# Moving the last column tile of each layer's input projection behind the index matmuls, in a two-block transformer kernel

## The chip, the cores and the metric

The kernel runs on one core of a Trainium2 chip. The metric is the device time of one execution in microseconds, lower is better. Engines: TensorE (PE, matmuls; PEld its weight loads), VectorE (DVE), ScalarE (ACT), GpSimd (POOL) and SyncE (SP, which here only issues DMAs). Each engine works through its own queue in order, and waits on semaphores that the others raise.

## What is computed

A first transformer block (three attention branches, a recurrent branch, gates, a dense feed-forward) is followed by two layers of a second kind. The change is in those two layers. For 256 tokens of width 1024, each of them computes

```
h = x @ w_in                          # 1024 x 1892, split into
a_q a_k a_v  b_q b_k b_v  i_q i_k i_w  c_q c_kv c_kr
o_a: sliding-window attention of rope(a_q), rope(a_k), a_v
o_b: the indexer: score = sum_h i_w * relu(rope(i_q) . rope(i_k)); the 64 best keys
     of each query are kept; attention of rope(b_q), rope(b_k), b_v over those keys
o_c: q_c = rms_norm(c_q) @ w_uq, kv_c = rms_norm(c_kv) @ w_ukv, attention with rope parts
x = layer_norm(alpha*x + [o_a o_b o_c] @ w_out)
x = layer_norm(alpha*x + mixture_of_experts(x))
```

All in float32. Products are made of three matmuls of split operands: a value is rounded to a short form ("hi"), the rest is kept apart ("lo"), and hi*hi, hi*lo and lo*hi are added up.

## The kernel before

**Weight tiles.** All weights stream in tiles of 128 x 2048 through a ring of three buffers. SyncE loads a tile into `raw`, ScalarE rounds it into `whi` (`split_hi`, L1197 to L1202), VectorE writes the difference into `wlo` (`split_lo`, L1543 to L1547), TensorE uses both and raises `tile_used`. A rounding waits until the tile three places earlier has been used. The load of a tile waits until the tile three places earlier has been split by both engines.

**The input projection.** The 1892 columns of `w_in` are eight tiles of 256 columns (the last of 100) taken in the order `L_COLS = [0, 1, 2, 4, 5, 6, 7, 3]`: tile 3, columns 768 to 1023, is the B queries and comes last (j = 7). `cols_tile` (L739) makes one: 2 token halves x 8 depths x 3 matmuls = 48 matmuls into PSUM bank 0 or 1 by turns. ScalarE evicts each into `h` (`evac_h`, L1395) and raises `ring_free`. Tiles 8 and 9 of the layer's ring are the up projections of the C branch, tiles 10 to 13 `w_out`, 14 the router.

**The order of the work** is written out by hand, for each engine, and is the same in both layers:

- TensorE (L967 to L989): column tiles 0 to 5, transposes of the A queries (L955), tile 6, transposes of the A keys and the rest, tile 7 (the B queries), then the wait for the rope of the index queries and for the eviction of the previous transposes, the transposes of the index queries, the wait for their eviction, and eight index matmuls (L987), which contract over 64 rows. Then it waits for the relu (L1014) and goes through twelve attention units of scores (L794), transposes of the probabilities (L806) and values (L821); between them stand the transposes of the C input at unit 1, the up projections at units 2 and 3 (L992 to L1011), the C transposes at 5 and 6, and the B transposes at unit 8.
- ScalarE (L1412 to L1426): evictions of the column tiles and of the transposes (`block_out`, L1402), each followed by the rounding of the tile two places on; behind the eviction of tile 7 the eviction of the index transposes (block 2), the relu of the index matmuls in two activations (L1424, L1425), and the rounding of tile 10. Then exponentials and evictions of the units.
- VectorE (L1782 to L1820): the subtractions of tiles 2 to 9, the moments of the C input, its scaling (L1808, needs GpSimd's power L706), the subtraction of tile 10, and behind the relu the eight index scores (L1819, each waits for the one before). Then unit 0: logits (L1572, L1574), a step of the top-64 search (L1826, L1827), and at unit 1 the lo part of the C input (L1833), for which TensorE's up projection waits.
- GpSimd (L696 to L718): rope of A, of the index part, of the C key part, the power L706, then behind the eighth `ring_free` of the layer (that is, the eviction of tile 7) the rope of the B queries and keys (L709; L676 to L679 and copies L687), and much later the rope of the C queries.

```
                pool.wait_ge(ring_free, l * 8 + (N_COL + 8))
                rope(5, 64, C_CC, C_SS, cols(BQ, 5), 4, [(1, BK)])
```

Of the kernel before, what the change touches and what calls it, by code (L numbers as in the profile page):

```python
# [192 lines left out]
def build(nc, I, out):  # L193
    with ExitStack() as ctx:
# [8 lines left out]
        def banks(a, b):  # L203
            return ps[:, a:b, :].rearrange("p a b -> p (a b)")
# [522 lines left out]
        def _(pe):  # L727
# [211 lines left out]
            for l in range(LAYERS):  # L939
# [12 lines left out]
                def turns(items, k=P):  # L952

                    for b, src in enumerate(items):
                        x = pe.transpose(banks(2, 4)[0:k, b * P:(b + 1) * P], src, ident)  # L955
                    x.then_inc(tb_full, 1)
# [7 lines left out]
                def doubled(which):  # L964
                    return [twice[which][:, t, :] for t in range(TT)]

                for j in range(8):  # L967
                    if j >= 2:
                        pe.wait_ge(ring_free, l * 8 + (N_COL + j - 1))
                    cols_tile(T_L + j, v, (N_COL + j) % 2, L_WIDTHS[j], True, (1,) if j < 2 else (0, 1))  # L970
                    if j == 5:
                        pe.wait_ge(rope_done, l * 4 + 1)
                        turns(pairs(AQ, 3))
                    if j == 6:
                        tb_wait(1)
                        turns([h[:, t, AQ + 384:AQ + 512] for t in range(TT)] + doubled(2) + doubled(3))
# [5 lines left out]
                for t, o, w in ((1, banks(4, 6), S), (0, banks(6, 7), P)):  # L982
                    for x in (0, 2, 1, 3):
                        a = 64 * (x % 2)
                        if x == 1:
                            lk(ins)
                        ins = pe.matmul(o[:, x * w:(x + 1) * w], iq_t[a:a + 64, x // 2, t * P:(t + 1) * P],  # L987
                                        ik_t[a:a + 64, 0:w], start=True, stop=True)
                ins.then_inc(idx_full, 1)  # L989


                def up_queries():  # L992
# [201 lines left out]
        def _(act):  # L1194
# [188 lines left out]
            for l in range(LAYERS):  # L1383
# [25 lines left out]

                one = lambda x: x.rearrange("p (a b) -> p a b", a=1)  # L1410
                sizes = [KD * min(256, IN2 - t * 256) for t in L_COLS] + [768, 512, TW, TW, TW, TW, 128, TW, TW]
                for j in range(9):  # L1412
                    if j >= 1:
                        evac_h(j - 1)
                    if j == 6:
                        block_out(0, [(aq_t[:, 0:3, :], 0, 6)])
                    if j == 7:
                        block_out(1, [(aq_t[:, 3:4, :], 0, 2), (ak_t, 2, 4)])
                    if j < 8:
                        split_hi(T_L + j + 2, v, sizes[j + 2])  # L1420
# [2 lines left out]
                act.wait_ge(pv_full, l * U_PER + U_L0)  # L1423
                act.activation(relu_t[0], banks(4, 6), ACT.Relu)  # L1424
                act.activation(relu_t[1], banks(6, 7), ACT.Relu).then_inc(idx_relu, 1)  # L1425
                split_hi(T_L + 10, v)  # L1426
                nu = l * U_PER + U_L0
                for i in range(U_PER + 2):
# [614 lines left out]
```

## Time and profile before

| | |
|---|---|
| time, median of 3 runs | 1383.97 us (1383.74 to 1385.13) |
| the profiled execution's own time | 1379.53 us |
| its span | 1377.7 us |
| mean granted clock of TensorE | 0.917 of full speed |
| busy: TensorE, VectorE, ScalarE, GpSimd | 1192.6, 782.8, 586.9, 104.0 us |
| bytes moved by DMA | 215.87 MB |

The span runs from the first to the last instruction of the profiled execution; its own time has a little around it. Busy time is the time in which an engine executes something, waits excluded. All times in rows below are microseconds from the start of the span, unless marked ns. "The chain that ended last" goes back from the last instruction, at each step to what released it. The granted clock has two levels here, 1.00 (2.4 GHz) and 0.50 (1.2 GHz); a window with a value between them holds a change.

### The profile page before, as it was taken

The numbers are of one execution on the slowest core, as the hardware profiler recorded it, in microseconds if no ns is written. First come the engines' busy times: TensorE is split into PE (matmuls) and PEld (weight loads), VectorE is DVE, ScalarE is ACT, GpSimd is POOL, SyncE is SP. The second block draws the span as 40 slices with busy tenths as digits, with TensorE's granted clock in tenths as the row PEclk, the third lists the DMA queues.
The fourth block names the chain that finished last, engine by engine and source line by source line (L and its number), as shares of the span: only waits on it lengthen the run. The fifth ranks groups of instructions, "written<-read, shape, count | busy, mean of one in ns | idle before, by whom it ended". The sixth has DMA issues, their size and how long they took to land.

```text
span 1377.7 us, 17333 instructions
## 1 busy us (share of the span) xinstructions
PE 1192.6 (87%) x6958; PEld 1040.3 (76%) x6958; DVE 782.8 (57%) x946; ACT 586.9 (43%) x706; POOL 104.0 (8%) x151
## 2 busy tenths in 40 slices
PE   4999899997999989868859999887958858998885
PEld 4999899987999979747657876666936747886664
DVE  5344545775444455465355467766367454557775
ACT  3444445633333333344124456553334314446661
POOL 3000101000000002610000000000621000000000
PEclk9999999998999998857969999998975978999997
DMA  8644434562555553300134569882410006468990
GB/s 270 211 144 123 151 122 150 175 209 99 195 183 183 184 175 97 114 19 1 31 121 153 182 219 312 307 294 85 144 54 3 31 31 213 136 200 284 309 317 37
DMA packets 115077, 215.87 MB, mean 157 GB/s; under 512 B 9546, under 2 KB 79178, under 8 KB 115008
## 3 DMA queue, kind: packets, MB, share of 16 engines
q1 hardware_dynamic: 112432, 209.90, 46.2%
q0 software_dynamic: 1424, 4.59, 1.0%
q8 instruction: 48, 0.79, 0.2%
q10 hardware_dynamic: 1152, 0.42, 0.1%
q14 instruction: 21, 0.17, 0.0%
HBM read 213.80 MB, written 1.09 MB: 156 GB/s over the span
## 4 chain that ended last, share of the span: by engine, by line
PE 66%; DVE 13%; DMA 9%; ACT 7%; issue 3%; POOL 1%; SPq 1%; POOLq 0%; ACTq 0%; DVEq 0%
PE ps L735 15%; PE ps L737 15%; PE ps L736 14%; DMA raw<-in_w_up 6%; DVE wlo L1546 6%; ACT whi L1202 4%; PE ps L794 3%; PE ps L771 3%; PE ps L821 3%; PE ps L772 3%; PE ps L773 3%; DMA raw<-in_w_down 2%; PE ps L806 2%; PE ps L1079 1%; PE ps L1080 1%
## 5 line engine op out<-in xcount | busy, mean ns | idle before, releaser
L1546 DVE TENSOR_TENSOR wlo<-raw,whi 128x2048 fp32r<-128x2048 f32 (+1 forms) x199 | 445.9, 2243 | 323.5 <-ACT whi L1202 322.6
L1202 ACT ACTIVATE whi<-raw 128x2048 fp32r<-128x2048 f32 (+1 forms) x199 | 369.5, 1861 | 227.2 <-PE ps L737 112.5
L735 PE MATMUL ps<-act_hi,whi 128*128 128x256 f32 (+1 forms) x784 | 228.1, 291 | 11.0 <-DVE act_lo L1553 11.0
L736 PE MATMUL ps<-act_lo,whi 128*128 128x256 f32 (+1 forms) x784 | 226.0, 288 | 0.0
L737 PE MATMUL ps<-act_hi,wlo 128*128 128x256 f32 (+1 forms) x784 | 225.9, 288 | 0.0
L735 PEld LDWEIGHTS ps<-act_hi,whi 128*128 128x128 f32 (+1 forms) x784 | 152.2, 194 | 17.3 <-DVE act_lo L1553 12.6
L736 PEld LDWEIGHTS ps<-act_lo,whi 128*128 128x128 f32 (+1 forms) x784 | 152.1, 194 | 1.2
L737 PEld LDWEIGHTS ps<-act_hi,wlo 128*128 128x128 f32 (+1 forms) x784 | 152.0, 194 | 1.0
L735 PE MATMUL ps<-whi,moe_r 128*128 128x512 f32 x320 | 132.8, 415 | 18.2 <-DVE wlo L1546 17.9
L737 PE MATMUL ps<-whi,moe_r 128*128 128x512 f32 x320 | 128.6, 402 | 0.0
L736 PE MATMUL ps<-wlo,moe_r 128*128 128x512 f32 x320 | 128.2, 401 | 0.0
L735 PE MATMUL ps<-whi,act_hi 128*128 128x256 f32 (+1 forms) x336 | 98.3, 293 | 4.5 <-DVE act_lo L1553 4.5
L735 PE MATMUL ps<-whi,mix_hi 128*128 128x512 f32 (+1 forms) x172 | 70.8, 412 | 32.5 <-DVE mix_lo L1833 13.7
L737 PE MATMUL ps<-whi,act_lo 128*128 128x256 f32 (+1 forms) x336 | 97.4, 290 | 0.0
L736 PE MATMUL ps<-wlo,act_hi 128*128 128x256 f32 (+1 forms) x336 | 97.3, 290 | 0.0
L735 PEld LDWEIGHTS ps<-whi,moe_r 128*128 128x128 f32 x320 | 61.4, 192 | 39.5 <-DVE wlo L1546 19.2
L628 POOL TENSOR_TENSOR small<-small 128x1 f32<-128x1 f32 x14 | 7.7, 557 | 946.9 <-DVE small L1564 946.8
L794 PE MATMUL ps<-arena 64*128 64x256 f32 (+3 forms) x208 | 63.3, 427 | 10.8 <-ACT pbuf L1425 3.2
L737 PEld LDWEIGHTS ps<-whi,moe_r 128*128 128x128 f32 x320 | 61.2, 191 | 14.9
L736 PEld LDWEIGHTS ps<-wlo,moe_r 128*128 128x128 f32 x320 | 61.6, 193 | 13.0
L735 PEld LDWEIGHTS ps<-whi,act_hi 128*128 128x128 f32 x336 | 67.1, 200 | 5.3 <-DVE act_lo L1553 5.3
L735 PEld LDWEIGHTS ps<-whi,mix_hi 128*128 128x128 f32 x172 | 33.6, 195 | 47.2 <-DVE mix_lo L1833 15.1
(258 smaller groups left out, 1945.8 us busy)
## 6 DMA issues: line engine op xcount, KB each, us to landing
raw<-in_w_in SPq DMA_DIRECT2D x45, 1024.0 KB, 5.5
raw<-in_w_down SPq DMA_DIRECT2D x43, 1024.0 KB, 5.0
raw<-in_w_gate SPq DMA_DIRECT2D x64, 512.0 KB, 4.4
raw<-in_w_up SPq DMA_DIRECT2D x64, 512.0 KB, 5.2
raw<-in_w_gu SPq DMA_DIRECT2D x22, 1024.0 KB, 5.1
raw<-in_w_out SPq DMA_DIRECT2D x12, 1024.0 KB, 4.9
raw<-in_p_b SPq DMA_DIRECT2D x2, 1024.0 KB, 5.2
raw<-in_p_c SPq DMA_DIRECT2D x2, 1024.0 KB, 5.3
```

Source lines behind the costliest of these rows:

```text
L735: pe.matmul(o, ah, bh, start=first, stop=False)
L736: pe.matmul(o, ah, bl, start=False, stop=False)
L737: return pe.matmul(o, al, bh, start=False, stop=last)
L771: pe.matmul(o, a, cc, start=f, stop=False)
L772: pe.matmul(o, a, d, start=False, stop=False)
L773: x = pe.matmul(o, b, cc, start=False, stop=g)
L794: x = pe.matmul(o[:, i, :], u["q"][i], u["k"][i], start=True, stop=True)
L806: x = pe.transpose(o[:, b * P:(b + 1) * P], p[:, i, kt * P:(kt + 1) * P], ident)
L821: x = pe.matmul(oo, pt[:, b * P:(b + 1) * P], u["v"][i][kt], start=f, stop=g)
L1079: pe.matmul(o, xk_hi[:, t, k, :], put[:, t, a:b], start=t == 0, stop=False)
L1202: act.activation(whi[:, c % 3, 0:n], raw[:, c % 3, 0:n], ACT.Copy).then_inc(hi_made, 1)
L1546: dve.tensor_tensor(wlo[:, c % 3, 0:n], raw[:, c % 3, 0:n], whi[:, c % 3, 0:n].bitcast(F32), ALU.subtract)\
```

## The change

In each of the two layers, TensorE's seven first column tiles stay where they are, and the eighth (the B queries) is issued behind the eight index matmuls, ahead of the wait for the relu. ScalarE no longer evicts it in the loop, but behind the two relu activations and ahead of the rounding of tile 10. Nothing else is changed: GpSimd's rope of the B queries waits for the same count of evictions, VectorE's and SyncE's queues are as before. No instruction is added or removed.

```diff
@@ TensorE @@
-                for j in range(8):
+                def columns(j):
                     if j >= 2:
                         pe.wait_ge(ring_free, l * 8 + (N_COL + j - 1))
                     cols_tile(T_L + j, v, (N_COL + j) % 2, L_WIDTHS[j], True, (1,) if j < 2 else (0, 1))
+
+                for j in range(7):
+                    columns(j)
                     if j == 5:
                         pe.wait_ge(rope_done, l * 4 + 1)
                         turns(pairs(AQ, 3))
...
                         ins = pe.matmul(o[:, x * w:(x + 1) * w], iq_t[a:a + 64, x // 2, t * P:(t + 1) * P],
                                         ik_t[a:a + 64, 0:w], start=True, stop=True)
                 ins.then_inc(idx_full, 1)
+                columns(7)
@@ ScalarE @@
-                for j in range(9):
+                for j in range(8):
                     if j >= 1:
                         evac_h(j - 1)
                     if j == 6:
...
                 act.activation(relu_t[0], banks(4, 6), ACT.Relu)
                 act.activation(relu_t[1], banks(6, 7), ACT.Relu).then_inc(idx_relu, 1)
+                evac_h(7)
                 split_hi(T_L + 10, v)
```

## Rows read from the trace of the kernel before

**Rows 1.** The page: its head, and the chain's shares by engine.
```profile
span 1377.7 us, 17333 instructions
...
PE 66%; DVE 13%; DMA 9%; ACT 7%; issue 3%; POOL 1%; SPq 1%; POOLq 0%; ACTq 0%; DVEq 0%
```

**Rows 2.** Chain that ended last, layer 0 (start, length, what); last, TensorE's timeline.
```profile
578.44 1.81 ACT whi L1202
580.27 2.29 DVE wlo L1546
...
586.11 0.70 DVE pbuf L1572
...
589.92 0.97 DVE mix_lo L1833
...
590.93 0.69 PE L735 MATMUL ps<-whi,mix_hi 128*128 128x384 f32 x1 [6.14 <-DVE mix_lo L1833]
```

**Rows 3.** Timeline of TensorE, layer 0 (start, length, line, form, count, idle before).
```profile
565.55 0.86 PE L955 MATMUL ps<-cst,arena 128*128 128x128 f32 x6
566.17 0.36 PE L735 MATMUL ps<-whi,act_hi 128*128 128x256 f32 x1
...
572.00 0.82 PE L955 MATMUL ps<-cst,arena 128*128 128x128 f32 x6
573.78 3.11 PE L987 MATMUL ps<-arena 64*128 64x256 f32 x16 [0.96 <-ACT arena L1407]
```

**Rows 4.** Timeline of ScalarE, layer 0.
```profile
566.45 0.87 ACT L1407 ACTIVATE arena<-ps 128x256 f32<-128x256 f32 x2 [0.36 <-PE ps L955]
...
572.20 0.60 ACT L1399 ACTIVATE arena<-ps 128x512 f32<-128x512 f32 x1 [4.36 <-PE ps L737]
572.86 0.87 ACT L1407 ACTIVATE arena<-ps 128x512 f32<-128x512 f32 x2
576.93 1.02 ACT L1424 ACTIVATE pbuf<-ps 128x1024 f32<-128x1024 f32 x1 [3.20 <-PE ps L987]
```

**Rows 5.** Timeline of GpSimd, layer 0: an index rope operation, then the B rope.
```profile
562.58 1.24 POOL L677 TENSOR_TENSOR arena<-arena,cst 128x160 f32<-128x160 f32 x1
...
573.80 0.85 POOL L676 TENSOR_TENSOR arena<-arena,cst 128x320 f32<-128x320 f32 x1
...
576.92 0.86 POOL L676 TENSOR_TENSOR arena<-arena,cst 128x320 f32<-128x320 f32 x1
...
579.74 0.52 POOL L687 COPY arena<-arena 128x128 f32<-128x128 f32 x2
```

**Rows 6.** Timeline of VectorE, layer 0: scalings of the C input, index scores.
```profile
573.93 3.06 DVE L1808 SCALAR_TENSOR_TENSOR arena<-arena,small 128x256 f32<-128x256 f32 x4 [1.05 <-POOL small L706]
...
582.48 0.86 DVE L1819 SCALAR_TENSOR_TENSOR arena<-pbuf,small,cst 128x256 f32<-128x256 f32 x2
583.38 2.69 DVE L1819 SCALAR_TENSOR_TENSOR arena<-pbuf,small,arena 128x256 f32<-128x256 f32 x6
```

**Rows 7.** Windows: us, PE, PEld, DVE, ACT, POOL busy, granted clock, DMA.
```profile
578.00:580.00 2.00, 1.45 (x3) 0.73 (x4) 0.00 (x0) 2.00 (x2) 1.86 (x5) 0.65 0.01 4
...
990.00:992.00 2.00, 2.00 (x18) 2.00 (x18) 0.16 (x1) 0.00 (x0) 1.89 (x3) 0.91 0.37 66
...
994.00:996.00 2.00, 2.00 (x14) 2.00 (x13) 0.14 (x1) 1.39 (x3) 1.26 (x6) 0.74 0.21 84
...
1008.00:1010.00 2.00, 2.00 (x10) 1.22 (x8) 1.40 (x1) 1.86 (x2) 0.25 (x2) 0.67 0.00 0
```

**Rows 8.** Timeline of ScalarE, layer 1.
```profile
994.44 0.87 ACT L1407 ACTIVATE arena<-ps 128x256 f32<-128x256 f32 x2 [0.98 <-PE ps L955]
...
1006.66 1.91 ACT L1202 ACTIVATE whi<-raw 128x2048 fp32r<-128x2048 f32 x1
```

**Rows 9.** Timeline of TensorE: scores of a unit at half and at full clock.
```profile
603.64 2.49 PE L794 MATMUL ps<-arena 64*128 64x256 f32 x4
...
643.93 1.45 PE L794 MATMUL ps<-arena 64*128 64x256 f32 x4
```

## The prediction

> **What bounds the kernel now.** I read the page first, then the chain that ended last around the first place the change touches (layer 0, 565 to 591 us), then each engine's timeline there, the two-microsecond windows with the granted clock, and the same place in layer 1. The page gives a span of 1377.7 us with two thirds of the chain on TensorE [rows 1]. That average says little about this spot. In the chain the reader is to see that after the relu (L1424 and L1425) the work which sets the end is not TensorE's: ScalarE rounds weight tile 10 at 578.44, VectorE subtracts it at 580.27, then VectorE's eight index scores and the first logits at 586.11, then the normalised C input is split at 589.92 and only then TensorE starts the up projection at 590.93 [rows 2]. TensorE's own row there says that it had been idle for 6.14 us and that VectorE's mix_lo released it [rows 2]. So in this stretch VectorE's queue is the bound, and its first item is the subtraction of tile 10, which cannot start before ScalarE has rounded that tile. The eight scores stand behind it in the same queue, however early the relu is.
>
> **What moves on TensorE.** The last column tile is 48 dense matmuls: it starts at 566.17 and the next transposes issue at 572.00, 5.83 us [rows 3]. Without it between them, the transposes of the index queries (rope done, their turn comes at 566.2) wait for the eviction of the transposes before, which ends at 566.45 + 0.87 = 567.32 [rows 4]. From the start of the transposes to the start of their eviction it takes 572.86 - 572.00 = 0.86 us, and the eviction 0.87 us [rows 3, 4]: it would run from 568.3 to 569.1. The index matmuls start just behind it, at 569.2 instead of 573.78 [rows 3], 4.6 us early. The relu starts 576.93 - 573.78 = 3.15 us after them [rows 3, 4], at 572.3, and its two activations are over at 573.8 instead of 578.44. The moved tile runs from 572.3 for 5.83 us, its last matmul ends near 578.15.
>
> **What that does to ScalarE.** The eviction of the moved tile (0.60 us, [rows 4]) now stands ahead of the rounding of tile 10. It ends near 578.8, and the rounding starts there instead of at 578.44 [rows 2]: **0.35 us late**. The relu's 4.6 us go nowhere: VectorE gets to the scores only behind tile 10, and TensorE's unit 0 scores, which the earlier relu frees, end long before the logits of 586.11 ask for them. In layer 1 the same sum starts from an eviction that ends at 994.44 + 0.87 = 995.31 [rows 8]; adding 0.05, 0.86, 0.87, 0.05, 3.1, 5.83 and 0.6 us in the same order gives 1006.7 for the rounding, which started at 1006.66 [rows 8]: **nothing** there. Layer 1 loses less because the tile ran its first microsecond at half clock before.
>
> **What that does to GpSimd, and through it to VectorE.** The eviction also frees GpSimd's rope of the B queries. It ran from 573.80 to about 580.3: first half 573.80 to 576.92, second half 576.92 to 579.74, then two copies [rows 5]. Its users come at unit 8, some 50 us later, so its own delay is hidden. But it now starts at 578.9 and needs 2 x 2.82 + 0.5 = 6.2 us (the second half had VectorE out of its way): it runs beside tile 10's subtraction and the eight scores, which had VectorE with GpSimd idle. What that costs is visible beside its first half: VectorE's four scalings of the C input (two of 256, two of 128 elements) took 3.06 us there, while six scores of the same two sizes, with a wait after each, took 2.69 us alone [rows 6]. Four at that pace are 1.79 us, so 3.1 us of rope cost VectorE 1.27 us. The subtraction starts at 580.6, after 1.8 us of rope, and holds the rope off while it runs: an earlier rope operation of 160 elements took 1.24 us beside the subtraction of tile 8, longer than one of 320 elements takes alone (0.86) [rows 5]. So behind it 6.2 - 1.8 = 4.4 us of rope are left, against 3.6 us of scores. 4.4 / 3.1 x 1.27 = **1.8 us late per layer**. Bounds: 0, if the two never want the same thing at once, and 4.4, if every operation of the one shuts the other out. I take 1.8, because its row has the same kind of pair. The scalings, now without the rope beside them, gain their 1.3 us, but VectorE then waits for tile 10 anyway (nothing is won).
>
> The Trainium skill (SBUF — State Buffer, "Who interferes with whom") speaks against this change more strongly: a VectorE instruction with two SBUF inputs and a GpSimd instruction that reads SBUF hold a shared port in turn and the second to issue is fully blocked. By that rule the cost would be the upper bound, 4.4 us per layer, and the sum without the clock 9.2 instead of 3.95 us. The rows agree that they slow each other, but four scalings and four rope operations took 3.1 us together, less than one after the other (1.5 to 1.8 and 2.8 us), so the sum goes by the rows.
>
> **Other queues.** SyncE's loads of tiles 11 and 12 wait for tiles already split; the one of tile 13 waits for tile 10's subtraction, some 2 us later than now, and is wanted only after the attention units: nothing. Rope of the C queries on GpSimd follows kv_c's eviction, 25 us later: nothing. The wait of the up projection for all eight evictions is met at 578.8, before it is asked. No instruction is added or taken away.
>
> **The clock.** It is the term that the trace bounds least. The window from 578 has a mean of 0.65, so the clock fell at 578.6, after the index matmuls and the wait for the relu; in layer 1 the same reckoning gives a fall only at 1008.7, two operations further, and before that a low stretch from 991.6 to 995.0, which ended while the last column tile ran [rows 7]. With the tile away from there, TensorE stands idle twice (1.2 and 0.9 us) around six transposes and then runs index matmuls on 64 of 128 rows: the same kind of work after which the clock fell at 578.6, now ahead of 5.83 us of dense work on the path. Bounds per layer: no fall, 0; half clock through index matmuls and tile, 3.1 x 0.72 + 5.83 x 0.8 = 6.9 us (0.72 from four score matmuls that took 2.49 instead of 1.45 us [rows 9], 0.8 taken a little above it for dense ones). I take one low stretch like that of layer 1, 3.4 us, in one of the two layers: half of it is lost, **1.7 us**. Downstream, later starts can shift the low stretches of the attention units by a step either way; I count 0 and leave it to the range.
>
> **Sum.** Layer 0: 0.35 + 1.8; layer 1: 0 + 1.8; clock: 1.7. Together +5.65 us. The profiled execution took 1379.53 us for its span of 1377.7, 4.4 us under the median of the runs, 1383.97; against its own time the change gives 1385.2, against the median **1389.6 us**.
>
> **Rivals.**
> 1. Low clock over most of the moved work in layer 1: the rise at 995.0 was bought by the very tile that leaves [rows 7]. Then index matmuls (2.2 us more) and half of the tile (2.3 us) run slow: 3.95 + 4.5 to 6.9 = +8 to +11, 1392 to 1395 us. For: that rise. Against: layer 0 arrives with the full clock.
> 2. No collision worth naming: GpSimd's operations slip into the gaps that the waits between the scores leave. Then only 0.35 us is left, 1384.3 us, no change to be seen. Against: the scalings of rows 6, which are independent and still lost time; for: the scores have a gap after each.
> 3. Faster: the dense tile now stands directly before unit 0 and the C transposes, so the clock falls later than at 578.6. If that carries over to the low stretch of the attention units, four matmuls cost 1.45 instead of 2.49 us [rows 9], and if transposes and values together gain a little more than the scores do (an estimate), a unit takes some 2.3 us less. It decides from two units per layer on: 2 x 2 x 2.3 = 9.2 us against 3.95, 1378.7 us. Against: TensorE idles 6 to 8 us before the up projection either way [rows 2], and the clock fell at 578.6 after a shorter wait.
> 4. By the skill's rule above the place and sign are those of the forecast, and the full bound gives 1383.97 + 9.2 = 1393.2 us; as a mechanism of this kernel it is a score waiting for a whole rope operation each time, 4.4 us in all per layer. The overlap in rows 5 and 6 speaks against it.
>
> **How the numbers follow.** Forecast 0.50; rival 1 0.18; rival 4 0.10; rival 2 0.14; rival 3 0.08. The range takes in rival 2 at its lower end (1384.0) and the low clock with the collision at its upper (1396.0), and leaves out rival 3 and the tail of two low layers. About 0.2% (2.8 us) is what a measurement of this kernel can tell from no change. Slower by more: 0.50 + 0.18 + 0.10 = 0.78. Within: 0.14. Faster: 0.08.
>
> **What the profile of the changed kernel would show.** Right: index matmuls of layer 0 near 569.2; relu near 572.3; the moved tile directly behind them; tile 10's rounding behind the tile's eviction at 578.8 or later; the rope's first operation of 320 elements at the same time; scores on VectorE longer than 0.48 and 0.35 us; first logits about 2 us later than 586.11. Wrong: scores at their old length beside a running rope (rival 2); a half clock between 996 and 1006 that lasts (rival 1); the up projection in either layer starting no later than before, counted from the start of the first column tile (the forecast fails altogether).

## The result, and the profile after

| | before | changed |
|---|---|---|
| median of 20 runs of each, on the same chip | 1383.3 us (1375.9 to 1402.5) | 1412.5 us (1386.8 to 1429.5) |
| ratio with its 95% interval | | 1.0114 (1.0082 to 1.0146) |
| the profiled execution's own time, its span | 1379.53, 1377.7 us | 1399.33, 1397.5 us |
| mean granted clock in it | 0.917 | 0.902 |

The ratio leaves out runs that lie more than 1.5% above the fastest of their kernel (14 of the changed kernel's 20), so here it tells the smaller part of the loss, and the median of all runs is given beside it throughout. By the ratio, the 1383.97 us shown ahead of the prediction become 1399.7. The sign was forecast; the size was not: 1389.6 us was predicted, and the range ended at 1396.0.

The changed kernel is not only slower but uneven, and its time goes with the clock. Over its 20 runs the mean granted clock and the time have a correlation of -0.98: 0.911 was 1386.8 us, 0.902 was 1399 to 1402, 0.879 was 1422 to 1429, some 11 us for each hundredth.

The page of the changed kernel, its head, the granted clock in 40 slices, and the chain's shares by engine:

```profile
span 1397.5 us, 17333 instructions
...
PEclk9999999998999989857869999998765877999997
...
PE 65%; DVE 14%; DMA 9%; ACT 7%; issue 3%; POOL 1%; SPq 1%; POOLq 0%; ACTq 0%; DVEq 0%
```

The instruction count is the same and the shares have hardly moved [rows 1]. As ahead of the change, the averages say nothing of the place. Its timeline does; first TensorE in layer 0 (start, length, line, form, count, idle before):

```profile
568.43 0.84 PE L955 MATMUL ps<-cst,arena 128*128 128x128 f32 x6 [1.05 <-ACT arena L1411]
570.24 4.71 PE L990 MATMUL ps<-arena 64*128 64x256 f32 x16 [0.96 <-ACT arena L1411]
574.88 0.58 PE L735 MATMUL ps<-whi,act_hi 128*128 128x256 f32 x1
...
577.99 0.28 PE L737 MATMUL ps<-whi,act_lo 128*128 128x256 f32 x1
```

Layer 0 starts about a microsecond later in this execution (below), so 570.24 answers to the predicted 569.2. The index matmuls are where they were expected, but take 4.71 us instead of 3.11 [rows 3], and the matmuls of the moved tile come some 0.21 us apart up to 577.8 and 0.12 us apart from there on. The windows of the same stretch (us, busy PE, PEld, DVE, ACT, POOL, granted clock, DMA share, GB/s) show why:

```profile
568.00:570.00 2.00, 0.84 (x6) 0.64 (x6) 1.13 (x3) 1.49 (x4) 1.49 (x5) 1.00 0.38 156
570.00:572.00 2.00, 1.70 (x7) 1.10 (x9) 1.74 (x8) 0.19 (x1) 0.00 (x0) 0.77 0.56 137
...
576.00:578.00 2.00, 2.00 (x12) 2.00 (x12) 0.30 (x2) 0.50 (x2) 0.00 (x0) 0.52 0.00 0
```

The clock fell to its lower level at about 571.1, in the index matmuls, after two waits around six transposes, and rose at 577.9, well into the dense tile. (Inside a window with a value between the two levels, the time of the change follows from the mean: 0.77 is 1.08 us at 1.00 and 0.92 us at 0.50.) Before, it had fallen at 578.6, behind all of this. ScalarE in layer 0:

```profile
574.99 1.02 ACT L1428 ACTIVATE pbuf<-ps 128x1024 f32<-128x1024 f32 x1 [4.80 <-PE ps L990]
575.91 0.59 ACT L1429 ACTIVATE pbuf<-ps 128x512 f32<-128x512 f32 x1
582.26 0.60 ACT L1403 ACTIVATE arena<-ps 128x512 f32<-128x512 f32 x1 [5.76 <-PE ps L737]
582.75 1.90 ACT L1206 ACTIVATE whi<-raw 128x2048 fp32r<-128x2048 f32 x1
```

The eviction of the tile now stands ahead of the rounding of tile 10, as predicted, and the wait ahead of it (5.76 us) is TensorE's. VectorE and GpSimd behind it:

```profile
584.69 2.29 DVE L1551 TENSOR_TENSOR wlo<-raw,whi 128x2048 fp32r<-128x2048 f32 x1 [8.39 <-ACT whi L1206]
586.90 1.95 DVE L1824 SCALAR_TENSOR_TENSOR arena<-pbuf,small,cst 128x256 f32<-128x256 f32 x2
588.88 3.51 DVE L1824 SCALAR_TENSOR_TENSOR arena<-pbuf,small,arena 128x256 f32<-128x256 f32 x6
592.42 0.69 DVE L1577 SCALAR_TENSOR_TENSOR pbuf<-ps,cst 128x512 f32<-128x512 f32 x1
```

```profile
582.93 0.86 POOL L676 TENSOR_TENSOR arena<-arena,cst 128x320 f32<-128x320 f32 x1 [8.14 <-ACT arena L1403]
...
584.85 2.85 POOL L679 TENSOR_TENSOR arena<-arena 128x320 f32<-128x320 f32 x1
587.77 0.92 POOL L676 TENSOR_TENSOR arena<-arena,cst 128x320 f32<-128x320 f32 x1
```

The rope starts as soon as the tile is evicted, is held through VectorE's subtraction (2.85 us for an operation that takes 0.86), and then runs beside the scores: 1.95 + 3.51 us for what took 0.86 + 2.69 [rows 6]. That is the predicted collision.

In layer 1 the clock was low from 997.8, ahead of the transposes, to 1014.8, where half of the tile's matmuls were done. TensorE there, and the windows around the fall and the rise:

```profile
1002.06 1.51 PE L955 MATMUL ps<-cst,arena 128*128 128x128 f32 x6 [1.05 <-ACT arena L1411]
1004.53 5.51 PE L990 MATMUL ps<-arena 64*128 64x256 f32 x16 [0.96 <-ACT arena L1411]
```

```profile
996.00:998.00 2.00, 2.00 (x20) 2.00 (x19) 0.55 (x1) 0.00 (x0) 1.92 (x3) 0.94 0.24 61
998.00:1000.00 2.00, 2.00 (x11) 2.00 (x12) 0.00 (x0) 0.28 (x1) 0.87 (x3) 0.50 0.85 315
...
1014.00:1016.00 2.00, 2.00 (x15) 2.00 (x15) 0.00 (x0) 0.00 (x0) 0.00 (x0) 0.79 0.00 0
```

**Where the 19.8 us went.** To compare layers that start at different times, count from the layer's first column-tile eviction. These are its rows on ScalarE, the first logits of layer 1 on VectorE, and the transposes of the attention output on TensorE (L783), before the change:

```profile
533.88 0.60 ACT L1399 ACTIVATE arena<-ps 128x512 f32<-128x512 f32 x1 [1.89 <-PE ps L737]
656.84 1.52 PE L783 MATMUL ps<-cst,arena 128*128 128x128 f32 x7 [0.73 <-DVE arena L1592]
960.62 0.60 ACT L1399 ACTIVATE arena<-ps 128x512 f32<-128x512 f32 x1 [1.94 <-PE ps L737]
1014.44 0.69 DVE L1572 SCALAR_TENSOR_TENSOR pbuf<-ps,cst 128x512 f32<-128x512 f32 x1
1083.66 1.68 PE L783 MATMUL ps<-cst,arena 128*128 128x128 f32 x7 [0.73 <-DVE arena L1592]
```

and after it:

```profile
534.85 0.60 ACT L1403 ACTIVATE arena<-ps 128x512 f32<-128x512 f32 x1 [1.90 <-PE ps L737]
663.03 1.37 PE L783 MATMUL ps<-cst,arena 128*128 128x128 f32 x6 [0.73 <-DVE arena L1597]
966.99 0.60 ACT L1403 ACTIVATE arena<-ps 128x512 f32<-128x512 f32 x1 [1.94 <-PE ps L737]
1028.31 0.69 DVE L1577 SCALAR_TENSOR_TENSOR pbuf<-ps,cst 128x512 f32<-128x512 f32 x1
1103.16 1.11 PE L783 MATMUL ps<-cst,arena 128*128 128x128 f32 x4 [0.73 <-DVE arena L1597]
```

| us | before | after | later |
|---|---|---|---|
| layer 0: first eviction to first logits | 586.11 - 533.88 = 52.23 | 57.57 | +5.3 |
| layer 0: first logits to output transposes | 70.73 | 70.61 | -0.1 |
| layer 1: first eviction to first logits | 53.82 | 61.32 | +7.5 |
| layer 1: first logits to output transposes | 69.22 | 74.85 | +5.6 |
| everything else | 1131.7 | 1133.2 | +1.5 |

So 12.8 of the 19.8 us are lost ahead of the attention units, where the change is, and 5.6 inside those of layer 1, whose instructions are the same. "Everything else" holds the late start of 1 us; it is not explained, and is of the size in which executions differ (layer 0's first eviction stands between 532.6 and 535.7 in all eighteen profiles).

### The profile page after: what moved, and what is told of

It reads as the page before. It is cut to its first block, busy times and chain, and to the rows that moved or that the text cites. A ratio compares the mean times of both kernels' runs of the same rounds, so it can differ in the third digit from the quotient of the medians.

```text
span 1397.5 us, 17333 instructions
## 1 busy us (share of the span) xinstructions
PE 1202.3 (86%) x6958; PEld 1048.1 (75%) x6958; DVE 783.5 (56%) x946; ACT 587.5 (42%) x706; POOL 108.5 (8%) x151
## 4 chain that ended last, share of the span: by engine, by line
PE 65%; DVE 14%; DMA 9%; ACT 7%; issue 3%; POOL 1%; SPq 1%; POOLq 0%; ACTq 0%; DVEq 0%
PE ps L735 15%; PE ps L737 14%; PE ps L736 14%; DVE wlo L1551 6%; DMA raw<-in_w_up 5%; ACT whi L1206 4%; PE ps L794 3%; PE ps L821 3%; PE ps L771 2%; PE ps L772 2%; PE ps L773 2%; DMA raw<-in_w_down 2%; PE ps L806 2%; PE ps L1083 1%; PE ps L1084 1%
## 5 line engine op out<-in xcount | busy, mean ns | idle before, releaser
L735 PEld LDWEIGHTS ps<-whi,moe_r 128*128 128x128 f32 x320 | 61.4, 192 | 44.0 <-DVE wlo L1551 23.9
L737 PE MATMUL ps<-whi,mix_lo 128*128 128x512 f32 (+1 forms) x172 | 69.4, 404 | 0.0
```

Of the source, the lines that this page charges most:

```text
L735: pe.matmul(o, ah, bh, start=first, stop=False)
L737: return pe.matmul(o, al, bh, start=False, stop=last)
```

## The experiments

Each experiment starts from the kernel before or from the changed one, as its heading says. The kernels with extra matmuls write results that nobody reads and that later matmuls overwrite; they are there for TensorE's activity alone. Every group of four has its own runs of the kernel before on its own chip: 35 with a median of 1380.75 us for the first, 17 with 1382.25 for the second, 28 with 1381.52 for the third, 35 with 1381.23 for the fourth. The first and the third group ran on one chip, the second on another and the fourth on a third. The changed kernel without further edits ran only in the first comparison and in the second group, so a difference of a few microseconds between groups can also be the chip's.

**First group: one part of the loss at a time, from the changed kernel.** The rope held back until unit 0's probabilities are under way, after the scores (GpSimd):

```diff
                 pool.wait_ge(ring_free, l * 8 + (N_COL + 8))
+                pool.wait_ge(l_ready, l * U_PER + (U_L0 + 1))
                 rope(5, 64, C_CC, C_SS, cols(BQ, 5), 4, [(1, BK)])
```

> The changed kernel, but GpSimd's rope of the B queries also waits for the first logits of unit 0, so it no longer runs beside the subtraction of tile 10 and the eight index scores. Collision theory: the eight scores take 3.6 us from the first start to the logits again instead of 5.4, in both layers; 1.8 us less per layer, 3.6 us less in all than the changed kernel, its low clock unchanged. Rival, that the scores are slow for another reason (they read what the relu wrote, or tile 10 is late): they stay at 5.4 us. By the Trainium skill (SBUF - State Buffer, Who interferes with whom) the two engines shut each other out for whole instructions; that rule would also take the 5.4 us down to 3.6.

The scores ahead of the subtraction of tile 10 (VectorE):

```diff
-                split_lo(T_L + 10, v)
                 dve.wait_ge(idx_relu, l + 1)
...
+                split_lo(T_L + 10, v)
```

> The changed kernel, but VectorE makes the eight index scores ahead of the subtraction of tile 10 instead of behind it. Theory, that the earlier relu is worth nothing only because VectorE's queue holds tile 10 in front of the scores: the scores run while TensorE is still on the moved tile, before the rope starts, take 3.6 us, and the first logits follow the subtraction at once: some 5.4 us earlier per layer than in the changed kernel, about 11 us less in all, 1388 us or a little less where the changed kernel is at 1399. Rival, that the chain is held by TensorE's low clock and the tile itself: the logits still wait for the tile, so at most the 5.4 us of the scores per layer can come back, and nothing below the kernel before is possible while the clock falls.

Half of the moved tile put back, so that TensorE has dense work ahead of the index transposes:

```diff
+                columns(7, (0,))
                 pe.wait_ge(rope_done, l * 4 + 2)
...
-                columns(7)
+                columns(7, (1,))
```

> The changed kernel, but the first 24 matmuls of the moved tile (the first token half) run ahead of the index transposes, in the time in which TensorE waits for an eviction; the other 24 stay behind the index matmuls. Clock theory (two waits around six transposes and then index matmuls on half the rows bring the clock down): the granted clock stays high through the index matmuls in layer 0, where it fell at 571.5, and tile 10 is rounded near 578 instead of 582.8; the collision stays. About 5 us less than the changed kernel in layer 0, 8 or more in layer 1 if it holds there too; 1386 to 1392 us. Rival, that the index matmuls alone bring the clock down: it falls during them all the same and only the 1 us of filled wait is won per layer.

The whole tile left behind, and the two waits around the index transposes filled with 8 and 6 dense matmuls:

```diff
+                def filler(n):
+                    for k in range(n):
+                        pe.matmul(ps[:, (N_COL + 7) % 2, 0:256], act_hi[:, k, 0:P], act_hi[:, k, :], start=True, stop=True)
+
+                pe.wait_ge(ring_free, l * 8 + (N_COL + 6))
+                filler(8)
                 pe.wait_ge(rope_done, l * 4 + 2)
...
+                filler(6)
```

> The changed kernel with dense matmuls added whose results are overwritten: eight ahead of the index transposes and six behind them, one microsecond or less each at full clock, in the two waits of TensorE for evictions. No other work moves. Clock theory: the clock holds, the index matmuls take 3.1 us instead of 4.7 and 5.5, the tile 5.8 instead of 7.2 and 8.1; some 3 us less than the changed kernel in layer 0 and 4 to 8 in layer 1, 1388 to 1392 us. Rival, that it is the index matmuls on half the rows and not the waits: no change, or slower by the fillers where they run at half clock (up to 2 us).

| | ratio (95%) | median of all |
|---|---|---|
| rope later | 1.0070 (1.0040 to 1.0101) | 1390.6 |
| scores first | 1.0045 (1.0010 to 1.0081) | 1383.7 |
| half before | 1.0013 (0.9981 to 1.0044) | 1381.6 |
| fillers | 1.0031 (0.9985 to 1.0078) | 1386.7 |

Half before was expected at 1386 to 1392 us and fillers at 1388 to 1392: both medians lie below, as does that of scores first (1388 expected). The 3.6 us less than the changed kernel that were expected of rope later can't be read here, since that kernel did not run in this group; the two rows can.

Rope later, VectorE in layer 0: the scores are back at their old lengths, and the collision is gone.

```profile
587.52 0.87 DVE L1825 SCALAR_TENSOR_TENSOR arena<-pbuf,small,cst 128x256 f32<-128x256 f32 x2
588.42 2.69 DVE L1825 SCALAR_TENSOR_TENSOR arena<-pbuf,small,arena 128x256 f32<-128x256 f32 x6
```

Fillers, layer 1: first column-tile eviction (ScalarE), index matmuls (TensorE), scores and first logits (VectorE), and a window over the index matmuls.

```profile
960.38 0.60 ACT L1410 ACTIVATE arena<-ps 128x512 f32<-128x512 f32 x1 [1.94 <-PE ps L737]
...
995.76 3.11 PE L997 MATMUL ps<-arena 64*128 64x256 f32 x16 [0.25 <-ACT arena L1418]
...
1009.49 1.95 DVE L1831 SCALAR_TENSOR_TENSOR arena<-pbuf,small,cst 128x256 f32<-128x256 f32 x2
1011.47 3.51 DVE L1831 SCALAR_TENSOR_TENSOR arena<-pbuf,small,arena 128x256 f32<-128x256 f32 x6
1015.02 0.69 DVE L1584 SCALAR_TENSOR_TENSOR pbuf<-ps,cst 128x512 f32<-128x512 f32 x1
```

```profile
996.00:998.00 2.00, 1.94 (x12) 1.15 (x11) 1.73 (x8) 0.00 (x0) 0.00 (x0) 1.00 0.76 231
```

This layer is the cleanest reading of the case. The clock never fell ahead of the scores, the index matmuls take 3.11 us again, and the first logits come 1015.02 - 960.38 = 54.64 us after the first eviction. Before, an undisturbed layer needed 52.23 (layer 0 of the kernel before; 52.2 again in the old-order layers of the second group). The new order by itself thus costs **2.4 us per layer**: 1.9 in the scores, 0.5 in the eviction ahead of the rounding. What the changed kernel needs beyond that, 57.57 and 61.32, is clock. In layer 0 of the same execution the low stretch came earlier, over the fillers themselves (563.5 to 570.4), and the first logits at 57.21: there they kept the index matmuls at 3.11 us and brought the first logits no earlier.

Two of the other profiles hold something that no theory had. Rope later, TensorE in the B units at the end of each layer's attention; layer 0, then layer 1:

```profile
646.00 1.45 PE L795 MATMUL ps<-arena 64*128 64x256 f32 x4
...
648.81 1.45 PE L795 MATMUL ps<-arena 64*128 64x256 f32 x4
...
1078.00 2.49 PE L795 MATMUL ps<-arena 64*128 64x256 f32 x4
...
1083.07 2.49 PE L795 MATMUL ps<-arena 64*128 64x256 f32 x4
```

A unit takes 2.81 us in layer 0 and 5.07 in layer 1. Windows of the same execution:

```profile
641.00:651.00 10.00, 9.07 (x61) 7.14 (x60) 8.49 (x24) 6.25 (x21) 0.00 (x0) 0.98 0.01 2
...
1070.00:1080.00 10.00, 9.19 (x39) 7.94 (x37) 6.50 (x19) 4.28 (x15) 0.00 (x0) 0.50 0.00 1
```

TensorE is over nine tenths busy in both, and the clock came back in the one (50 us behind the first logits) and not in the other, where it stayed low for 95.6 us, to 1112.5. From first logits to output transposes layer 0 took 70.6 us and layer 1 84.2. I call this a missed rise: **some 13.5 us per layer**. The same stood in layer 1 of scores first and of half before. The profiled executions of these three took 1405.2, 1396.0 and 1397.3 us, 12 to 16 us above their medians, which is the size of one miss. Half before is the plainest of them: in its layer 1 the clock did not fall until 1013.0, the index matmuls ran at the full clock, and the rise was missed all the same. Its index matmuls, and a window in the missed stretch:

```profile
999.57 3.11 PE L991 MATMUL ps<-arena 64*128 64x256 f32 x16 [0.96 <-ACT arena L1412]
```

```profile
1070.00:1080.00 10.00, 9.94 (x39) 8.32 (x38) 5.42 (x15) 3.35 (x12) 0.00 (x0) 0.50 0.01 2
```

**Second group: in which layer, and all three edits at once.** The changed kernel itself again, the change in layer 0 alone, in layer 1 alone, and the changed kernel with rope later, scores first and half before together. The edit for layer 0 alone:

```diff
-                for j in range(7):
+                late = l == 0
+                for j in range(7 if late else 8):
...
-                columns(7)
+                if late:
+                    columns(7)
```

(the same `late` on ScalarE; `l == 1` in the other kernel)

> The changed kernel itself, unaltered, on the same chip as the next three, since its times spread over 43 us in the first comparison. Theory: the spread is that of the granted clock (its runs' mean granted clock went from 0.878 to 0.911, the time from 1429 to 1387 us), the ratio to the kernel before lies again between 1.008 and 1.015 or above. Its profile again has index matmuls of 4 to 5.5 us in at least one layer and scores of 5.5 us in both.

> The column tile is moved in layer 0 only; layer 1 is as in the kernel before. Theory: the loss splits as in the two traces: 5 us here (1.8 of it the collision, some 3 the low clock over index matmuls and tile), so 0.3 to 0.5% over the kernel before. Rival, that layer 1's long low stretch in the attention units comes by chance, whatever is moved: some of its runs are then as slow as those of the changed kernel.

> The column tile is moved in layer 1 only; layer 0 is as in the kernel before. Theory: the larger part of the loss, 10 to 14 us, 0.7 to 1.0% over the kernel before: 1.8 us of collision, 7 to 8 us by the low clock over index matmuls and tile, and the rest by a longer low stretch in its attention units. Rival: both layers lose alike, 0.4 to 0.6%.

> The changed kernel with the three edits together: half of the tile ahead of the index transposes, index scores ahead of the subtraction of tile 10, rope of the B queries behind the first logits. Theory: the scores are over before tile 10 comes, the logits follow its subtraction at once, no collision, and the clock mostly holds: first logits 2 to 4 us earlier per layer than in the kernel before, 0.2 to 0.5% faster than it. Rival, that the clock in the attention units decides and moves at random: within 0.2% of the kernel before.

| | ratio (95%) | median of all | first logits to output transposes, layers 0, 1 |
|---|---|---|---|
| changed again | 1.0239 (1.0191 to 1.0286) | 1413.5 | 84.3, 83.6 |
| layer 0 only | 1.0157 (1.0127 to 1.0187) | 1403.0 | 84.3, 69.8 |
| layer 1 only | 1.0109 (1.0052 to 1.0167) | 1403.4 | 69.2, 70.7 |
| all three edits | 1.0017 (0.9972 to 1.0063) | 1402.0 | 84.2, 84.2 |

The granted clock in 40 slices on the page of the changed kernel again, then of all three edits:

```profile
PEclk8999999999999989655869999998765587999998
```

```profile
PEclk8999999998999999755869999998955677999998
```

The changed kernel's median agrees with the 1412.5 us of the first comparison, while its lowest run was 1386.8 there and 1408.8 here, so that the two ratios differ. Its profiled execution missed the rise in both layers and took 1429.3 us. Each layer alone costs two thirds of what both do (medians 20.8 and 21.2 us above 1382.25, together 42 against 31.3), so with six runs each they do not add up: what a layer loses seems to depend on more than its own edit. For layer 0 alone 0.3 to 0.5% had been expected, and it lost 1.6%; the expected split between the layers is not there. And the three edits together, whose first logits stand at 49.4 us, 2.8 *ahead* of the kernel before, still ran from 1373.5 to 1407.5 us with a median 1.4% above it. In its profile the local cost is repaired and the missed rise stays; 0.2 to 0.5% faster had been expected. Each of its three edits alone had medians of 1381.6 to 1390.6 us in the first group, on the other chip; whether the three together or the chip bring the 1402.0 is not settled.

**Third group: dense work inside the attention stage.** 24 matmuls at unit 5, while TensorE waits for the C input, in the changed kernel and in the kernel before; in the latter also 24 more ahead of the up projection, in the wait for the lo part of the normalised C input, and that with scores first and rope later on top.

```diff
+                def keep_warm(n):
+                    for k in range(n):
+                        pe.matmul(ps[:, 0, 0:256], act_hi[:, k % KD, 0:P], act_hi[:, k % KD, :], start=True, stop=True)
...
+                        pe.wait_ge(ring_free, l * 8 + (N_COL + 8))
+                        keep_warm(24)
...
+                        pe.wait_ge(ukv_sb, l * 4 + 4)
+                        keep_warm(24)
```

> The changed kernel with 24 dense matmuls added per layer, results overwritten, in the 4 us in which TensorE waits at unit 5 for GpSimd's kcat. Theory: the second and larger part of the loss is that the granted clock misses its rise in the attention units (some 50 us behind the first logits in some layers, never within the stage in others), which costs 13 us in a layer where it misses. The fillers let it rise at unit 5 or 6 in every layer: from the first logits to the transposes of the output 70 us or less instead of 71 to 84, all runs within some 10 us, 1.5 to 2.5% less than the changed kernel, near the kernel before. Rival, that the rise depends on something else: the low stretches stay and the fillers cost 1 to 2 us a layer.

> The kernel before with the same 24 fillers at unit 5. Theory: its layers rise 49 to 51 us behind the first logits, with the fillers they rise some 15 us earlier; units 5 to 7 at full clock save 4 to 8 us per layer: 0.6 to 1.2% faster than the kernel before, and with less spread. Rival as above: 0.1 to 0.3% slower.

> The kernel before with 24 fillers ahead of the wait for mix_lo (TensorE idle for 6 us there) as well as at unit 5. Theory: the up projection of the queries runs at full clock, 1.8 us less, and units 2 and 3 partly: 1 to 3 us per layer less than with the fillers at unit 5 alone. Rival: the clock has fallen again by unit 5 and nothing is added.

> The kernel before (tile in its old place) with both groups of fillers, index scores ahead of the subtraction of tile 10, and the rope of the B queries behind the first logits. Theory: the scores start when the relu is over, while ScalarE rounds tile 10, and the first logits follow the subtraction by nothing: 1.5 to 2 us less per layer than with the fillers alone, 1 to 1.8% faster than the kernel before.

| | ratio (95%) | median of all |
|---|---|---|
| changed, 24 at unit 5 | 1.0135 (1.0094 to 1.0176) | 1400.2 |
| before, 24 at unit 5 | 0.9993 (0.9966 to 1.0021) | 1381.9 |
| before, 24 and 24 | 0.9946 (0.9919 to 0.9974) | 1374.4 |
| before, 24 and 24, scores first, rope later | 0.9953 (0.9923 to 0.9983) | 1376.1 |

Before with 24 and 24, TensorE in layer 0 (the 24, and the first matmul of the up projection behind them), and windows:

```profile
587.38 5.06 PE L994 MATMUL ps<-act_hi 128*128 128x256 f32 x24
593.73 0.44 PE L735 MATMUL ps<-whi,mix_hi 128*128 128x384 f32 x1 [1.29 <-DVE mix_lo L1841]
```

```profile
602.00:619.00 17.00, 16.14 (x61) 13.09 (x60) 11.19 (x28) 7.91 (x20) 5.83 (x12) 0.50 0.04 4
619.00:649.00 30.00, 24.20 (x173) 20.30 (x173) 20.67 (x58) 16.22 (x53) 0.00 (x0) 1.00 0.00 1
```

The 24 end 1.3 us ahead of the up projection, so they cost nothing, and the up projection now runs at the full clock; in layer 0 the low stretch of the attention is 17 us long instead of 37.5 (599.1 to 636.6 before). From first logits to output transposes a layer takes 64.1 and 66.0 us instead of 70.7 and 69.2. With 24 at unit 5 alone the kernel before gains nothing, where 0.6 to 1.2% had been expected: in layer 0 the clock rose at 620.1, fell again at 626.9 and came back only at 640.6 (636.6 without them), and the stage took 70.8 us. The changed kernel's median is 12 to 13 us lower with them than in the two comparisons without, and its profiled execution missed no rise. That does not show that they bought it: the comparison with the second group goes across chips, and rope later had 1390.6 on this chip without them. Scores first and rope later on top of 24 and 24 brought the first logits 1.8 us earlier per layer (50.4 us behind the first eviction), as expected, and no time: the stages behind them took 72.3 and 68.5 us instead of 64.1 and 66.0. It had been expected 1 to 1.8% faster than the kernel before and was 0.5%. So the coupling between an earlier edit and the clock in the attention stage is not a thing of the moved tile alone.

**Fourth group: fillers at both places.** The changed kernel with all three edits and 24 and 24; the changed kernel with the 8 and 6 of the first group and 24 and 24; the same with rope later; and before with 24 and 24 once more as its yardstick.

> The changed kernel with half of the tile ahead of the index transposes, index scores ahead of the subtraction of tile 10, the rope of the B queries behind the first logits, and both groups of 24 fillers. Theory: with the clock kept up in the attention units this is the order that gives the first logits earliest (49.4 us behind the first eviction of the layer, against 52.2 in the kernel before): 0.2 to 0.4% faster than the kernel before with both groups of fillers, 0.7 to 1% faster than the kernel before. Rival: any order in which the index matmuls follow waits costs the clock its level; then no better than the kernel before with fillers.

> The changed kernel with fillers in all the waits that matter: eight and six around the index transposes, 24 ahead of mix_lo and 24 at unit 5. What is left of the change with the clock held: tile 10 rounded 0.4 us late in layer 0, and the collision of 1.9 us per layer; first logits 54.6 instead of 52.2 us behind the first eviction. 4 to 6 us (0.3 to 0.4%) slower than the kernel before with both groups of fillers. If it is over 0.8% slower, something besides clock, queue order and collision is missing from the account.

> As the one before, with the rope of the B queries also behind the first logits. Only the 0.4 us in layer 0 is left: within 0.2% of the kernel before with both groups of fillers; 3.8 us less than the same without this wait.

> The kernel before with both groups of 24 fillers, once more, beside the three kernels that it is to be compared with: 0.4 to 0.7% faster than the kernel before, as in its first comparison.

| | ratio (95%) | median of all | first logits to output transposes, layers 0, 1 |
|---|---|---|---|
| three edits, 24 and 24 | 0.9963 (0.9936 to 0.9989) | 1378.2 | 75.1, 74.0 |
| changed, 8, 6, 24 and 24 | 1.0069 (1.0049 to 1.0090) | 1392.6 | 74.9, 74.3 |
| the same, rope later | 1.0024 (1.0000 to 1.0047) | 1385.8 | 70.3, 70.0 |
| before, 24 and 24, again | 0.9945 (0.9915 to 0.9975) | 1374.1 | 69.1, 63.2 |

Three things follow.

The collision has its price in the time as well. Taking the rope away from the scores gains 6.7 us in the medians of one group; in the two profiled executions it brings the first logits 1.95 us earlier in layer 0 and 1.94 in layer 1, 3.9 in all. The rest lies in the attention stages (4.6 and 4.3 us shorter in these two executions).

The gain of before with 24 and 24 repeats, 0.55% after 0.54%. No version of the changed kernel did better; three edits with 24 and 24 (0.9963, where 0.7 to 1% had been expected) is the nearest, and their intervals overlap.

The order stays dear with all these fillers, and the fillers did not hold the clock. The changed kernel with all of them is 1.2% above before with 24 and 24 (1.0069 against 0.9945), some 17 us, where 4.8 come from the order, and the expectation called more than 0.8% a sign that something is missing. With rope later it is still 0.8% above, where 0.2% had been expected. In the profiled executions (1404.0 us, the highest of its twelve runs, and 1374.2) its first logits are 0.9 and 5.4 us late, and the two attention stages 5.8 and 11 us longer. A window over most of layer 1's stage, first the changed kernel with all fillers, then before with 24 and 24:

```profile
1030.00:1090.00 60.00, 47.96 (x208) 39.53 (x208) 38.88 (x107) 26.05 (x77) 5.83 (x12) 0.64 0.01 2
```

```profile
1020.00:1080.00 60.00, 48.37 (x275) 39.41 (x273) 39.40 (x111) 30.80 (x90) 5.83 (x12) 0.84 0.04 11
```

From first logits to output transposes the clock was low for 58 and 54 us in the one and for 35 and 20 us in the other. Over all runs the mean granted clock was 0.916 against 0.926, and at the 11 us for each hundredth of the first comparison (an estimate) that is some 10 of the 17 us. So what is left beside the order is mostly the clock at the lower level again. Why the late tile leaves it there, with dense work in both waits, is not explained.

## Why the prediction was wrong in its size

- **What bounds the place: right.** The rounding of tile 10, its subtraction, the scores and the first logits stay the chain. The relu of layer 0 ended 2.9 us earlier than before, counted from the layer's first eviction (575.91 + 0.59 - 534.85 = 41.65 against 44.56; 4.6 were expected), and that bought nothing.
- **What moves on TensorE: right in its order and start, wrong in its lengths**, since both durations (3.1 and 5.83 us) were taken from a stretch with the full clock. Index matmuls started where forecast (570.24 less 0.97 is 569.27, forecast 569.2).
- **Eviction ahead of the rounding: right.** 0.35 us predicted in layer 0 and nothing in layer 1; with the clock at its full level 2.4 - 1.9 = 0.5.
- **The collision: right.** 1.8 us per layer predicted from the pace of four scalings beside the rope, 5.46 - 3.55 = 1.9 measured (1.95 + 3.51 against 0.86 + 2.69). The range 0 to 4.4 was wide, and the nearest row chose well in it. The Trainium skill (SBUF — State Buffer, "Who interferes with whom") would have the later of the two fully blocked. The trace agrees for the big subtraction (GpSimd's operation took 2.85 us and ended behind it), and not for the scores: 3.9 us of rope stood beside them and cost 1.9. Rival 4 has fallen.
- **The clock: this step failed.** It said "I take one low stretch like that of layer 1, 3.4 us, in one of the two layers: half of it is lost, 1.7 us." Both layers had one. In layer 0 it was 6.8 us long (571.1 to 577.9), the index matmuls took 1.6 us more and the tile 1.5; in layer 1 it was 17 us long (997.8 to 1014.8) and cost 0.7 at the transposes, 2.4 at the index matmuls and 2.3 at the tile. That is 3.1 + 5.4 = 8.5 us where 1.7 were counted, and inside the bound of 6.9 per layer that the text gave. Taken from the first logits it is 2.9 and 6.7 us (57.57 and 61.32 less 54.64), the fall in column tile 6 included; the kernel before had lost 1.6 us in layer 1 to its own low stretch (53.82 against 52.23). The argument against rival 1, "layer 0 arrives with the full clock", was true and no protection: it arrived with it and lost it in the index matmuls.
- **Downstream: this step failed too.** "I count 0 and leave it to the range" priced a shift of the low stretches at nothing. In the profile it was 5.6 us in layer 1; in other executions a whole missed rise, 13.5 us in that layer. Nine of the changed kernel's 20 runs took more than 1421 us, and only one less than 1395. In the changed kernel again (1429.3 us) it was 13.5 and 14.4 us, of 50 in all. No execution near the median (29 us lost) was profiled, so its share there is not shown. The range had no place for this term: it left out "the tail of two low layers", and low clock in both layers was the common case.
- **Rivals.** Rival 1 named the mechanism, the low clock over the moved work, but in layer 1 alone; it happened in both. Rival 3 had the right size for a unit (2.3 us; 5.07 - 2.81 = 2.26) and the wrong sign. The dense tile in front of unit 0 did put the fall off, from 7.5 and 5.7 us ahead of the first logits (586.11 - 578.6, 1014.44 - 1008.7) to 4.2 and 3.2 (592.42 - 588.2, 1028.31 - 1025.1), but the clock was low at the up projection all the same.

What the runs show of the downstream term, and what they leave open. Over all profiled executions, 8 of the 16 layers with a late tile (whole or half) and no fillers at unit 5 missed the rise, none of the 4 layers in the old order, and none of the 16 with fillers at unit 5 (8 in either order). Five of the eight were in the second group, on its chip. That the change makes the miss more frequent fits the times (medians +29 and +31 us in two comparisons, with the mean clock down); which property of it does is not shown. A low clock at the index matmuls is not needed: half before missed in layer 1 after index matmuls at the full clock, and with all three edits it was low there for 3.4 us at most (the index matmuls took 3.51 and 3.18 us), and both layers missed. Nor is a late start of the units, which there was early. I found no rule by which the offset of the first logits, from 49.4 to 61.4 us, tells which layer misses.

One thing in the traces goes with it. In 9 of the 20 layers without fillers at unit 5, the first fall of the clock in the stage came more than 4.0 us ahead of the first logits, both layers of the kernel before among them, and none of the nine missed. In the other 11 it came later (from 3.9 us ahead to 2.5 behind); eight missed, and a ninth, layer 1 of the changed kernel, stayed low for 54.6 us instead of 34 to 38. The late dense tile puts this fall off. That would tie the miss to the change, but it was read from the traces afterwards, two of the late falls recovered as usual, the nearest two layers on either side are 0.2 us apart, and no run sets the time of the fall by itself.

## What to carry to other kernels

Moving dense work behind small matmuls and waits also moves the clock: cost the moved instructions at both levels of the granted clock, and take the low one as the likely case where the new neighbours are the kind that stood ahead of a fall. Where a kernel's later stage runs long at the low level, an edit far ahead of it can cost more there than where it is made; look at the windows of that stage in several executions, and at the spread of the times, before putting a zero. An engine that is freed early gains nothing if the queue of the bound has another item in front, and a helper released late (here the rope) may run into that bound.

## What the hardware showed that I had not expected

- The clock fell while TensorE was busy without a gap: in layer 1 at 997.8, in column tile 6 (100 columns), with 2.00 of 2.00 us busy in the window from 996 and in each of the four before it. Idle time is not the only thing ahead of a fall.
- It stayed at the lower level for 95.6 us (1016.9 to 1112.5) in one layer and for 37.6 us (603.9 to 641.5) in the other of the same execution, with the same instructions and about the same busy share (9.19 and 9.07 of 10 us where they part). Half before has a window of 10 us with 9.94 busy at the lower level. In the two kernels compared here, the profiled executions shown first have the rise 49 to 51 us behind the first logits (such as 642.8 - 592.4 = 50.4); where it is missed, it comes in the output projection.
- One kernel's runs spread over 43 us (1386.8 to 1429.5) with the mean granted clock from 0.911 to 0.878. The kernel before spread over 27.
- 48 matmuls per layer with results that nobody reads, in waits that were there anyway, made the kernel before 0.54% and 0.55% faster (intervals 0.9919 to 0.9974 and 0.9915 to 0.9975).
